# Feed-forward runs of a two-layer decoder step: the first output block's rounding, its low part and the first gate sums moved ahead

## What is computed

```
def swiglu_ffn(h, w_in, w_out):
    g, u = jnp.split(h @ w_in, [D_FF], axis=-1)
    return (jax.nn.silu(g) * u) @ w_out
...
        yp = yp + swiglu_ffn(rmsnorm(yp, norm_ffn[i]), w_ffn_in[i], w_ffn_out[i])
        ys = ys + swiglu_ffn(rmsnorm(ys, norm_ffn[i]), w_ffn_in[i], w_ffn_out[i])
```

## Time and profile before

| | |
|---|---|
| median of 3 runs | 1286.08 us (1284.96 to 1286.16) |
| the profiled execution | 1286.95 us, span 1285.1 us |
| PE busy, VectorE, ScalarE, GpSimd | 1260.3, 785.1, 576.6, 427.0 us |
| granted clock of PE | 0.997 over the span |
| read from HBM | 136.46 MB |

### The profile page before, as it was taken

The page is one execution under the profiler, slowest core; times in us unless marked ns, Lnnn a source line. Parts: engine busy times, 40 slices in busy tenths (PEclk is TensorE's granted clock), DMA queues, the critical chain, the costliest instruction groups (busy, mean ns, idle before and its releaser), DMA issues.

```text
span 1285.1 us, 23305 instructions
## 1 busy us (share of the span) xinstructions
PE 1260.3 (98%) x9438; PEld 1211.6 (94%) x9438; DVE 785.1 (61%) x1361; ACT 576.6 (45%) x1037; POOL 427.0 (33%) x250
## 2 busy tenths in 40 slices
PE   9999999999999999999999999999999999999997
PEld 8888999999999999999889999899999999999996
DVE  5776757972277316658446787678961466317655
ACT  5565545562277415743023454225461366317631
POOL 1000033423322332236565544464323322232150
PEclk9999999999999999999999999999999999999998
DMA  9411122273277425743232332223263277416632
GB/s 328 162 34 50 51 67 77 73 163 91 70 177 160 129 83 122 164 117 117 77 104 87 116 125 97 86 78 119 81 150 92 86 159 166 124 66 155 143 106 74
DMA packets 50569, 145.43 MB, mean 113 GB/s; under 512 B 7088, under 2 KB 11120, under 8 KB 49024
## 3 DMA queue, kind: packets, MB, share of 16 engines
q1 hardware_dynamic: 33968, 107.30, 25.9%
q0 software_dynamic: 12960, 23.60, 11.0%
q10 hardware_dynamic: 3536, 13.05, 2.8%
HBM read 136.46 MB, written 9.44 MB: 114 GB/s over the span
## 4 chain that ended last, share of the span: by engine, by line
PE 83%; DVE 6%; DMA 4%; issue 3%; ACT 2%; POOL 1%; SPq 1%; ACTq 0%; DVEq 0%
PE ps L689 26%; PE ps L691 25%; PE ps L690 25%; DMA wlo<-w_blocks_in 1%; PE ps L819 1%; PE ps L866 1%; DMA more_lo<-w_blocks_in 1%; POOL wlo L640 1%; PE ps L842 1%; DMA sinks<-sinks_in 1%; PE ps L1150 1%; PE ps L1157 1%; DMA wst<-w_blocks_in 1%; DVE S L1874 1%; DVE more_lo L1578 0%
## 5 line engine op out<-in xcount | busy, mean ns | idle before, releaser
L640 POOL TENSOR_TENSOR wlo<-wst,whi 128x1024 fp32r<-128x1024 f32 x100 | 249.3, 2493 | 346.4 <-ACT whi L2126 343.7
L689 PE MATMUL ps<-hid,whi 128*128 128x288 f32 x704 | 208.9, 297 | 2.8 <-POOL wlo L640 2.8
L689 PE MATMUL ps<-xhi,whi 128*128 128x288 f32 x688 | 209.0, 304 | 1.1 <-DVE wlo L1371 0.7
L690 PE MATMUL ps<-hid,whi 128*128 128x288 f32 x704 | 208.2, 296 | 0.0
L691 PE MATMUL ps<-hid,wlo 128*128 128x288 f32 x704 | 208.0, 295 | 0.0
L690 PE MATMUL ps<-xlo,whi 128*128 128x288 f32 x688 | 202.9, 295 | 0.0
L691 PE MATMUL ps<-xhi,wlo 128*128 128x288 f32 x688 | 202.2, 294 | 0.0
L2126 ACT ACTIVATE whi<-wst 128x1024 fp32r<-128x1024 f32 x66 | 69.8, 1058 | 168.4 <-PE ps L691 168.4
L689 PEld LDWEIGHTS ps<-xhi,whi 128*128 128x128 f32 x688 | 129.0, 187 | 9.6 <-issue 8.3
L689 PEld LDWEIGHTS ps<-hid,whi 128*128 128x128 f32 x704 | 132.6, 188 | 4.3 <-POOL wlo L640 4.2
L691 PEld LDWEIGHTS ps<-hid,wlo 128*128 128x128 f32 x704 | 132.3, 188 | 0.0
(11 more groups left out here) (288 smaller groups left out, 3045.7 us busy)
## 6 DMA issues: line engine op xcount, KB each, us to landing
wst<-w_blocks_in SPq DMA_DIRECT2D x188, 512.0 KB, 3.5
wlo<-w_blocks_in POOLq DMA_DIRECT2D x60, 256.0 KB, 4.4
more_lo<-w_blocks_in POOLq DMA_DIRECT2D x30, 256.0 KB, 5.1
S<-s_in ACTq DMA_DIRECT2D x4, 1024.0 KB, 5.0
s_sample_out<-S ACTq DMA_DIRECT2D x4, 1024.0 KB, 4.4
y_out<-x SPq DMA_DIRECT2D x16, 144.0 KB, 1.8
bias<-bias_in SPq DMA_DIRECT2D x1, 2048.0 KB, 11.1
x<-x_in SPq DMA_DIRECT2D x4, 288.0 KB, 7.0
```

The source lines that it names most:

```text
L640: nc.gpsimd.tensor_tensor(lo, wst[:, slot, :], raw(hi), ALU.subtract).then_inc(w_split, 1)
L689: mm(out, stat[0], mov[0], start=start, stop=False, skip_group_check=skip)
L690: mm(out, stat[0], mov[1], start=False, stop=False, skip_group_check=skip)
```

## The change

In each run's last pair ScalarE rounds the run's first output block directly behind copy 5, no longer behind A22; GpSimd makes its low part before it issues A22's transfer, no longer after it. In each run's first pair ScalarE takes A11 of the next pair ahead of S4 and S3, and S3 behind copy 5. In the first run of a layer VectorE does both gate sums of tile 4 ahead of S2's sum for the next pair, and S1's low part ahead of tile 3's hidden low part. Nothing is added or left out.

```diff
@@ gpsimd, ffn @@
                     for f in fs:
                         if f != fs[-1]:
                             quarter_low("A11", l, f + 1)
+                        else:
+                            split(DOWN_AT[l][ph][0])
                         quarter_low("A22", l, f)
                         if f != fs[-1]:
                             quarter_low("A12", l, f + 1)
-                    for n in DOWN_AT[l][ph]:
+                    for n in DOWN_AT[l][ph][1:]:
                         if n < B_LAST:
                             split(n)
@@ vector, ffn @@
                 sum_s1(N_DIRECT + 1)
+                gate_left(N_DIRECT)
+                gate_right(N_DIRECT)
                 sum_s2(N_DIRECT + 1)
+                sum_low("S1", N_DIRECT + 1)
                 hidden_low(3)
-                sum_low("S1", N_DIRECT + 1)
                 operand_low("T4")
...
-                        gate_left(f)
-                        gate_right(f)
+                        if f > N_DIRECT:
+                            gate_left(f)
+                            gate_right(f)
@@ scalar, ffn @@
                         copy(1, f)
-                        if f == fs[0]:
-                            for q in ("S4", "S3"):
-                                quarter_high(q, f)
                         if more:
                             quarter_high("A11", f + 1)
+                        if f == fs[0]:
+                            quarter_high("S4", f)
                         copy(5, f)
+                        if f == fs[0]:
+                            quarter_high("S3", f)
+                        if not more:
+                            late_split(n0)
                         if f > fs[0] or f == N_DIRECT:
                             hidden_high(f - 1)
                         quarter_high("A22", f)
-                        if not more:
-                            late_split(n0)
                         copy(6, f)
```

## The result

The changed kernel takes 1298.59 us (median of four runs, 1297.37 to 1300.42); the kernel before, timed beside it, 1285.52 us. The ratio is 1.0105, with a 95% interval of 1.0087 to 1.0122: slower by 13.1 us. The profiled execution took 1299.15 us, its span is 1297.3 us. The two profiled executions lie 12.2 us apart. The direction was forecast; the size was not, and 1298.59 lies 4.1 us above the range.

What follows compares the result with a forecast made beforehand. PE, busy 98% of the span, was taken as the bound, so only its waits count. First pairs -4.1 and later adds +8.5 gave +4.4 us on 1286.08, so 1290.5 us; range 1282.0 to 1294.5.

Steps and rivals of the forecast that it cites:

- The last pairs' mechanism: At six run ends, two PE waits vanish, but product 4 still waits for A22's add, delayed by two loads issued together.
- The two waits that go: Last pairs: waits for copy 6 and the output block's GpSimd low part, 1.37 us each time, 8.2 in six, costed at nothing.
- The landing: Last pairs: A22's add lands after 6.55 us against 5.13, 1.4 us later, 8.5 us in six; bounds 0 and 11.4.
- -4.1 + 8.5: Whole kernel: first pairs win 4.1 us, the later add at the six ends costs 8.5, net +4.4 us.
- The first pairs: Earlier A11 and gate sums: 1.48 + 1.17 + 0.3 in later runs, 0.6 per layer's first run; 4.1 us won, between 2 and 4.6.
- five waits: PE's waits before the change for low-part transfers of A11, the adds into wlo: 3.3 us in all.
- a load alone lands in 4.1 us: DMA queues: landing time taken for an undisturbed load, against 6.9 us for a load and add waiting together.
- The upper bound: Slow end of the sum: 1.9 us at each end, 11.4 in all, less 2 won, gives 1295.5.
- Add first: Rival, chance 0.25: at run ends the second load does not disturb the add; only first pairs count, 1282.0 us.
- small disturbance: Rival, chance 0.17: the add lands 0.2 to 0.9 us later at each end; 1285.3 us, no change to be told.
- everything pays: Rival, chance 0.04: A22's transfer starts or lands 1.6 us earlier at the ends; 9.8 + 4.1 us go, 1272 us.

Runs made afterwards that it cites:

- the run that fills the wait: Changed kernel plus 18 unread matmuls at each run's end, between the first output block's two slices and the last pair's product 4: 1292.9 us, ratio 1.0065.
- the version with the subtraction: Changed kernel with A22's low part of each run's last pair made by GpSimd's own subtraction instead of the transfer: 1274.57 us, ratio 0.9917.

## Why the prediction was right and wrong

**The last pairs' mechanism: right.** The two waits that go, their worth taken as nothing because A22's chain does not move, the two loads that go out together, the add late by them, waits of about 3 us (2.54 to 2.88): each is in the trace, and holding back one load gives 15.2 us back.

**The landing: right.** 1.4 us for each end was forecast, 1.29 measured, 7.7 us instead of 8.5.

**The sum: wrong by a term that it did not have.** This is the step that failed: "-4.1 + 8.5" prices the later landing as the time by which product 4 starts later and nothing else. Behind a wait that grows to 2.5 to 2.9 us the next matmuls may run at the lower clock: 6.5 us in the profiled execution, and 5.1 to 5.7 by the run that fills the wait. The trace of before could not price it: its three shorter waits at each run's end stand apart, with matmuls between them and no fall behind. But the forecast itself named waits of about 3 us as its sign and put nothing for what comes behind them, in the sum or in the range. Removing the first two waits joins the idle time into one piece, and that alone did not do it: with one load held back, five joined waits of 1.14 to 1.60 us left the clock up. It took the later landing on top. Without the lower clock the same sum, with 2.1 and 7.7 as measured, gives 1291.7, inside the range.

**The first pairs: mis-sized.** 2.1 us measured by itself, 4.1 forecast. The later runs' waits for A11 went (2.95 us by the terms of the sum, at the edge of the measured 0.9 to 3.0; 1166.00 and 1028.59 have no counterpart among PE's waits). The 0.6 us for each first run did not come: in layer 0 VectorE's sum for product 4 starts at 262.07 instead of 262.40, and 0.29 us of these 0.33 were there long before the pair began (a wait of PE among the direct tiles, 0.46 us long in both, ends at 210.27 before and at 209.98 now).

```profile
262.40 0.45 DVE L1609 TENSOR_TENSOR h<-ps,kept 128x288 f32<-128x288 f32 x1
...
262.07 0.45 DVE L1611 TENSOR_TENSOR h<-ps,kept 128x288 f32<-128x288 f32 x1
```

I had VectorE's sum right as the obstacle but not that the time won would be handed on, from A11 to the up half, from there to copy 1, from there to the next pair's add.

**The whole.** Forecast -4.1 + 8.5 = 4.4; by the runs -2.1 + 7.7 + 5.1 to 6.5 = 10.7 to 12.1; measured 13.1, with an interval of 11.2 to 15.7. So 1.0 to 2.4 us of the median stay unexplained. Between the two profiled executions, 12.2 us apart, the terms nearly close: 7.7 + 6.5, less 2.95 for the A11 waits that went, and 1.1 (0.81 idle and 0.27 of restart) for a wait that the kernel before does not have, for A12's transfer in layer 0's third run. That makes 12.3. Why this transfer came late is not shown.

```profile
556.04 0.40 PE L691 MATMUL ps<-bhi,whi 128*128 128x288 f32 x1 [0.81 <-DMA wlo<-w_blocks_in]
```

**Smaller slips.** Of the "five waits" in the earlier trace rows put down to A11's transfer, one of 0.18 us, at 1099.23, is for A12's. And "a load alone lands in 4.1 us" was read from a load with the add 0.22 us behind it; one with nothing issued beside it for 2.3 us (263.47) took 3.5. Neither moves the sum. The upper bound worked out to 1295.5 while the range ended at 1294.5; the measured time lies beyond both.

**The rivals.** "Add first" fails: the add is issued before the second load and lands behind it. The Trainium skill, "DMA: Bandwidth & Descriptors", section on queues, rings and completion order, says that each DMA engine takes turns between the queue rows that have work, packet by packet. By that rule alone the second load would not have moved the add; the landings of 4.1, 5.1 and 6.4 us with no, one and two loads say that each load of 512 KB around the add costs it 1.0 to 1.3 us, the one issued 0.16 us behind it too. The "small disturbance" fails with the 1.29 us. That "everything pays" needs A22 to come sooner: the version with the subtraction does that, and at 1274.57 is near the 1272 that I gave for it.

## What to carry to other kernels

When a change removes a stall, look for the transfer that the stall was covering and for every load that the earlier release will start: the price stands in the queue of another engine. When short waits of TensorE go and one long one takes their place, ask for the clock behind it as well: here pieces of 1.80 us or less cost nothing there and pieces of 2.13 to 2.88 us mostly did. Where a transfer of some 5 us is what an engine ends up waiting for, look whether an idle engine can make the same data in 2.

## What the runs showed of the hardware

The clock: behind the waits of 2.50 to 2.88 us for this add (twelve, in the changed kernel and in the one with the last-pair part) the granted clock was at the lower level 8 times and stayed up 4 times; behind one of 2.13 us it fell, and behind none of 1.80 us or less in the runs told here. A wait of the same length can go either way (2.86 us stayed up, 2.88 fell; 2.54 stayed up, 2.50 fell), so such a loss belongs into a range and not only into a sum.

The load and the add: GpSimd's 256 KB add landed after 4.0 to 4.2 us with no load beside it and after 6.2 to 6.6 us between two loads of 512 KB in the changed kernel and in the one with the last-pair part (up to 7.9 in the version with the filled wait), the later of which, issued 0.16 us behind it, landed 1.3 us ahead of it in the changed kernel.

GpSimd's subtraction of 128x512 took 1.33 us at the first end in one order and 1.81 us in another. In the slower one 0.65 us of it lie beside VectorE's hidden low part, in the faster one 0.19 us. That hidden low part took 0.76 us before, with GpSimd idle, and 1.43 us in the changed kernel beside GpSimd's block. That the two slow each other down fits these numbers; no run here parts it from other causes.
